# Taking each pair of whole expert units ahead of four split units instead of two, in a mixture-of-experts decoder kernel

## The reference

```python
logits = (t @ w_router)
top_v, top_i = lax.top_k(logits, 2)
top_w = softmax(top_v)
combine = sum(one_hot(top_i, 8) * top_w[..., None], axis=1)
for e in range(8):
    out += combine[:, e:e+1] * ((silu(t @ w1[e]) * (t @ w3[e])) @ w2[e])
```

## Time and profile before

| what | value |
|---|---|
| median of 3 runs | 1240.68 us (1237.93 to 1241.63) |
| the profiled execution | 1240.51 us |
| its span, first to last instruction | 1238.9 us |
| mean granted TensorE clock | 0.999 |
| TensorE busy | 1214.2 us, 98% of the span |
| VectorE busy | 816.3 us, 66% |
| ScalarE busy | 663.0 us, 54% |
| moved by DMA | 393.73 MB, 318 GB/s over the span |

### The profile page before, as it was taken

How to read it: one execution, slowest core, us unless ns; L and a number is a source line. 1 busy time by engine, 2 the same in 40 slices (tenths; PEclk the granted TensorE clock), 3 DMA queues, 4 the chain that set the end, 5 groups by cost and what they waited for, 6 DMA issues and landing times. The chain is left out here.

```text
span 1238.9 us, 15727 instructions
## 1 busy us (share of the span) xinstructions
PE 1214.2 (98%) x6167; PEld 933.2 (75%) x6167; DVE 816.3 (66%) x788; ACT 663.0 (54%) x682; POOL 81.1 (7%) x76
## 2 busy tenths in 40 slices
PE   9999999999999999999999999999999999999994
PEld 8778888888888878888777776667777666777761
DVE  6867766656455766769776776666766676676632
ACT  7567445444336566457565555555555555555520
POOL 0600002000001501010000000000000000000000
PEclk9999999999999999999999999999999999999999
DMA  9753448745545454459999999999999999999996
GB/s 378 291 204 132 174 170 313 298 176 198 188 152 207 169 172 154 161 202 346 421 420 421 420 422 419 403 422 421 421 420 422 421 418 411 423 422 421 420 418 244
DMA packets 56734, 393.73 MB, mean 318 GB/s; under 512 B 6704, under 2 KB 6704, under 8 KB 11632
## 3 DMA queue, kind: packets, MB, share of 16 engines
q1 hardware_dynamic: 53104, 374.84, 76.0%
q0 software_dynamic: 3408, 17.57, 3.8%
q10 hardware_dynamic: 144, 0.26, 0.1%
HBM read 386.35 MB, written 13.64 MB: 323 GB/s over the span
## 5 line engine op out<-in xcount | busy, mean ns | idle before, releaser
L558 DVE TENSOR_TENSOR wl<-raw,wh 128x2048 fp32r<-128x2048 f32 x251 | 577.3, 2302 | 293.9 <-ACT wh L547 293.3
L547 ACT ACTIVATE wh<-raw 128x2048 fp32r<-128x2048 f32 x251 | 481.0, 1918 | 327.9 <-PE ps L565 178.5
L563 PE MATMUL ps<-wh,XT_h 128*128 128x512 f32 x944 | 375.5, 398 | 0.3 <-DVE wl L558 0.3
L565 PE MATMUL ps<-wh,XT_l 128*128 128x512 f32 x944 | 368.3, 390 | 0.0
L564 PE MATMUL ps<-wl,XT_h 128*128 128x512 f32 x944 | 367.7, 390 | 0.0
L563 PEld LDWEIGHTS ps<-wh,XT_h 128*128 128x128 f32 x944 | 177.3, 188 | 45.1 <-issue 8.6
L565 PEld LDWEIGHTS ps<-wh,XT_l 128*128 128x128 f32 x944 | 177.2, 188 | 38.0
L564 PEld LDWEIGHTS ps<-wl,XT_h 128*128 128x128 f32 x944 | 177.4, 188 | 34.6
L1690 PE MATMUL ps<-raw,few_X 128*64 128x256 f32 x1056 | 123.9, 383 | 4.1 <-DMA raw<-in_units 4.0
L1690 PEld LDWEIGHTS ps<-raw,few_X 128*64 128x64 f32 x1056 | 72.8, 137 | 49.7 <-issue 14.4
L563 PE MATMUL ps<-wh,moe_gT_h 128*128 128x512 f32 x220 | 88.4, 402 | 0.0
(11 more groups left out here) (288 smaller groups left out, 974.6 us busy)
## 6 DMA issues: line engine op xcount, KB each, us to landing
raw<-in_units SPq DMA_DIRECT2D x350, 1024.0 KB, 10.3
x_rows<-in_zeros POOLq DMA_DIRECT2D x8, 512.0 KB, 8.9
y_rows<-in_zeros POOLq DMA_DIRECT2D x6, 512.0 KB, 20.0
raw<-in_boot SPq DMA_DIRECT2D x5, 512.0 KB, 7.2
y_rows<-xs POOLq DMA_DIRECT2D x5, 512.0 KB, 8.2
back<-x_rows POOLq DMA_DIRECT2D x4, 512.0 KB, 9.2
h<-in_x SPq DMA_DIRECT2D x1, 1024.0 KB, 12.7
rows<-in_rows SPq DMA_DIRECT2D x1, 896.0 KB, 17.3
```

The source lines that it names most:

```text
L547: nc.scalar.activation(wh[:, U.split_slot(j), :], raw[:, U.raw_slot(j), :], ACT.Copy).then_inc(hi_ready, 1)
L558: nc.vector.tensor_tensor(wl[:, s, :], raw[:, U.raw_slot(j), :], wh[:, s, :].bitcast(F32), ALU.subtract).then_inc(lo_ready, 1)
L563: nc.tensor.matmul(o, xh, bh, start=start, stop=False)
L565: return nc.tensor.matmul(o, xl, bh, start=False, stop=stop)
```

## The change

When a pair of light units is put in, the loads stay as they are. In the order of use the pair is put before the last four units listed so far, where it was put before the last two. All of these four are heavy units.

```diff
--- before.py
+++ after.py
@@ -87,7 +87,7 @@
         while due - done >= 2:
             two = few[done:done + 2]
             loaded += two
-            used[-2:-2] = two
+            used[-4:-4] = two
             done += len(two)
     return loaded + few[done:], used + few[done:]
```

## The result

The changed kernel takes 1472.7 us (median of 4 runs, 1469.99 to 1476.02), the kernel before 1240.09 us (median of 4). The ratio is 1.189, with a 95% interval of 1.187 to 1.190. The profiled execution has a span of 1468.4 us and a mean granted TensorE clock of 0.941, where it was 0.999.

What follows compares the result with a forecast made beforehand. The experts' stage was taken as bound by transfers. A chain of 14.6 us less 10.2 us of cover leaves 4.4 us idle per pair; 43 pairs add 187 us to 1240.5, giving 1428 us, range 1380 to 1465.

Steps and rivals of the forecast that it cites:

- landing of b until H1 begins: TensorE's work on a pair's second light unit (b) before the next heavy unit (H1): 1.87 us plus 0.1 for transposes.
- H1 until the split that waits for it: From the first heavy unit after a pair to ScalarE's split start: 3.11 us plus 0.3 estimated for small operations.
- split until issue of the gated load: Split of the fourth heavy unit (H4) on both engines until SyncE issues the load wanting its raw slot: 4.43 us.
- issue until landing: Flight of the load with nothing ahead in the queue: 4.8 us by the row, against a skill-based estimate of 4.4.
- one turn: Experts' stage, distance from one light pair to the next: 18.5 us, where it was 14.1.
- What a load depends on: 43 loads, one per pair, now depend on a landing four loads earlier, as H4's split needs H1 used; before, six.
- The length of the chain: From a pair's second landing through use, split and issue to the gated load's landing: 14.6 us.
- about as long as the one that the clock outlasted there: TensorE's new pause of some 4 us compared with the program's end, where the clock stayed 1.00 until 1236 us.
- third rival: TensorE returns from each pause at half clock, 4.6 us more per chain: 1626 us, or 1478 in one of four; 6%.
- The excess without the clock: Experts' stage, DMA idle time per pair: chain 14.6 less cover 10.2, 4.4 us; 187 us over 43 pairs.
- What covers it: Four transfers, 10.2 us: the three loads still queued when the pair's second unit lands, and the gated load's own.
- The stage runs at the pace of the transfers: Experts' stage before the change: DMA and TensorE both full, transfers set the pace, one unit per 2.56 us.

Runs made afterwards that it cites:

- fill: Changed kernel plus 12 zero-adding TensorE matmuls before its wait for each pair's first unit: 1442.39 us, ratio 1.164.
- loads_too: Changed kernel with each pair also loaded two heavy units earlier, before the last two loads: 1238.98 us, ratio 0.9998.
- half: Changed kernel with only every second pair put before the last four units, the others before the last two: 1369.56 us, ratio 1.108.
- slots5_after: Changed kernel with 5 slots for raw units in place of 6: 1597.21 us, ratio 1.289.
- chain: Changed kernel plus 6 zero-adding matmuls in the middle of each pair's second light unit, behind its landing: 1548.98 us, ratio 1.252.
- chain_before: Kernel before plus 6 zero-adding matmuls in the middle of each pair's second light unit: 1304.16 us, ratio 1.052.
- lean_before: Kernel before with the middle of three products of each heavy unit left out in the experts' stage: 1238.38 us, ratio 0.999.
- k3: Changed kernel with pairs put before the last three units used instead of four: 1263.95 us, ratio 1.020.
- lean_three: Kernel before without the middle product of the experts' heavy units, and with pairs before the last three units: 1254.67 us, ratio 1.013.
- k1: Changed kernel with pairs put before the last one unit used instead of four: 1251.86 us, ratio 1.009.

## Why the prediction was wrong

The direction, the mechanism and most of the size held, but the time of 1428 us was 45 us short, and 1472.7 us lies 8 us above the range. The issues and landings of all 43 turns, read from the two traces, give each link as an average (us):

| link | forecast | changed kernel | pause filled (fill) |
|---|---|---|---|
| landing of b until H1 begins | 1.97 | 2.99 | 2.07 |
| H1 until the split that waits for it | 3.41 | 3.22 | 3.23 |
| split until issue of the gated load | 4.43 | 4.40 | 4.40 |
| issue until landing | 4.8 | 4.83 | 4.91 |
| chain | 14.6 | 15.4 | 14.6 |
| from there to the next pair's second landing | 3.8 | 4.0 | 4.2 |
| one turn | 18.5 | 19.5 | 18.8 |

(The forecast's 0.1 us for transposes stands in the first link, its 0.3 us for ScalarE's operations in the second.)

- **What a load depends on.** Right, and shown from three sides: the order of use alone costs nothing when the loads go along (loads_too), the price comes with each gated load (half, 6.2 us each), and one slot less costs a transfer for each pair (slots5_after).
- **The length of the chain.** All links but the first were right within 0.2 us, the landing by its row (4.8) and not by the estimate of 4.4 beside it. That the sum at a full clock came out at the 14.6 us of the forecast is partly luck: the 0.3 us allowed for ScalarE were 0.1, and two other links were each 0.1 longer. Work added between landing and issue is paid in full (chain).
- **The term that was mis-sized is the first link, b on TensorE: 1.87 us forecast, 3.00 us in the turn shown, 2.99 on average.** It was costed at the full clock. The step that failed is the reading that the new pause is "about as long as the one that the clock outlasted there": it took one pause at the end of the program as the measure for 43. There the clock fell 5.0 us after TensorE's last matmul. In the changed kernel it fell in 39 of 43 turns, 2.1 to 5.1 us after TensorE's last work; the four turns in which it stayed full had pauses of 2.9 to 3.6 us, and in others it fell with a pause of 2.7. So the one sample lay near the long end of the spread. I had the case as the third rival at 6%. Filling the pause gives 30 us back. Its price per pair was mis-sized too: I let b and H1 both run at half clock, 4.6 us, but the clock is back before H1 in every turn, and the runs give 30 / 43 = 0.7 us as an average. (The first link alone differs by 0.9 us between the two traces; the stretch behind the gated landing is 0.2 us shorter in the changed kernel.)
- **The excess without the clock** was forecast as 187 us (43 times the unrounded 4.36) and is 202 (fill), as the pairs are 18.8 and not 18.5 us apart. This lay within the bounds (150 to 215). The 0.3 us aren't in the chain, which has its 14.6 us, but behind it: the loads that follow the gated one take 4.2 us until the pair's second unit has landed, where 1.5 x 2.56 = 3.8 were reckoned. In 12 of the 43 turns the two light units landed over 3 us apart. Why wasn't looked into.
- **What covers it.** Four transfers: right, by slots5_after and the DMA share of 0.76. Three loads still queued when b lands: in 16 of the 43 turns there were only two, and the third went out later, but still ahead of the gated one, so that the count of four stands.
- **"The stage runs at the pace of the transfers"** was half the truth. Added work on TensorE is paid in full before the change (chain_before), less work gains nothing (lean_before). For the change at four it made no odds, as TensorE idles there. At three heavy units I had, from the same reading, expected no loss and found 25 us.
- **Signs in the profile.** DMA share 0.76 as said; 306 GB/s where I said about 320; 155.5 us of waiting for landings at L1690 where I said some 190 (43 pauses of 3.6 us, not 4; my "9" for before added the matmuls' and the weight loads' waits, 4.5 us is the matmuls' own); landing 8.6 us within 7 to 9.5; TensorE busy 1290.5 us and not 1214, since matmuls at half clock count longer.

The cause of k3's loss stays partly open. By the waits, the load behind the pair there depends on H4's split and this on H1, which TensorE now uses directly in front of the pair, so that only about one transfer of reserve is left for every delay of ScalarE or TensorE; the trace fits (one unit less in the queue, DMA share 0.99, 21 us more of waits for landings in a TensorE without spare time), and so does lean_three, but this was argued and not tested by itself. The reason given for k1's 13 us is read from its waits alone.

## What to carry to other kernels

When two orders share a ring, write down for each load which landing it depends on at nearest, through slots of every ring it passes; then compare the chain from that landing (use, split, issue, flight) with as many transfers as lie between. Here six transfers cover it and four don't, and a shift by one heavy unit more crosses the line at 5 us a turn. And where a new wait makes TensorE pause for some microseconds in every turn, cost what comes next at half clock as a case of real weight: one pause elsewhere that left the clock up proves little.

## What the hardware showed

A pause of 1.8 us in each 3.8 us left the clock at 1.00; pauses of 2.7 to 5.2 us, one in each turn of some 20 us, brought it down in 39 of 43 cases, in the pause or shortly after it. After the one of 3.79 us it was 0.50 over 920 to 923 us, so that a pair of light units took 5.39 us and not 3.67. Filling 2.84 us of the pause with matmuls whose moving operand is all zero kept the clock at 0.996 on average, so here such matmuls held it up.

A load of 1 MB with an empty queue in front of it took 4.8 us from issue to landing (4.83 on average over the 43 gated loads, most of them with an empty queue), and 10.6 us in the full queue of the kernel before.
